# Products of the identity with a constant at five steps of a chunk inverse, in a two-block transformer kernel

## The reference, cut to what matters

```python
def step(S, inp):
    w_t, k_t, v_t, a_t, b_t = inp[:5]
    sa = jnp.einsum('bhij,bhj->bhi', S, a_t)
    S = S * w_t[:, :, None, :] + sa[..., None] * b_t[:, :, None, :] + v_t[..., None] * k_t[:, :, None, :]
    y = jnp.einsum('bhij,bhj->bhi', S, inp[5]) if emit else None
    return S, y
```

## Time and profile before

| | |
|---|---|
| median of 3 runs | 2728.89 us |
| lowest, highest | 2722.32, 2736.04 us |
| the profiled execution | 2728.74 us, of which the profile's span is 2726.9 us |
| PE busy | 2439.7 us (89% of the span) |
| DVE, ACT, POOL busy | 943.1, 509.3, 133.9 us |
| the recurrence's inverses, on PE | from about 1393 to 1648 us of the span |

### The profile page before, as it was taken

How to read it: one execution, slowest core, us unless ns; L and a number is a source line. 1 busy time by engine, 2 the same in 40 slices (tenths; PEclk the granted TensorE clock), 3 DMA queues, 4 the chain that set the end, 5 groups by cost and what they waited for, 6 DMA issues and landing times.

```text
span 2726.9 us, 39043 instructions
## 1 busy us (share of the span) xinstructions
PE 2439.7 (89%) x16646; PEld 1745.4 (64%) x16646; DVE 943.1 (35%) x1712; ACT 509.3 (19%) x1072; POOL 133.9 (5%) x132
## 2 busy tenths in 40 slices
PE   8999899999999899999989999999777777777776
PEld 6868678887857788887658888854333333333333
DVE  3757624223734512322566642241111111111112
ACT  3116310001126211001235321021000000000002
POOL 1310000000310000000000000100000000000000
PEclk9999999999999999999989889999788788878788
DMA  8345357555332373462000004569999999999998
GB/s 331 152 195 221 127 198 269 193 229 229 129 139 78 131 273 148 177 249 103 31 1 2 2 3 186 217 277 428 428 428 428 429 429 428 428 428 429 428 429 355
DMA packets 48782, 667.04 MB, mean 245 GB/s; under 512 B 5530, under 2 KB 5573, under 8 KB 7568
## 3 DMA queue, kind: packets, MB, share of 16 engines
q1 hardware_dynamic: 46928, 657.81, 58.8%
q0 software_dynamic: 1728, 7.38, 0.8%
HBM read 664.11 MB, written 1.05 MB: 244 GB/s over the span
## 4 chain that ended last, share of the span: by engine, by line
PE 65%; DMA 26%; DVE 6%; ACT 2%; issue 1%; POOL 0%; DVEq 0%; SPq 0%; ACTq 0%; POOLq 0%
PE bank L2842 29%; PE bank L2818 20%; DMA arena<-exp_w 14%; DMA ring<-exp_w 11%; PE bank L2826 6%; PE bank L3112 2%; PE bank L3058 2%; DVE arena L2538 1%; PE bank L2830 1%; PE bank L2086 1%; DVE hT L2694 1%; PE bank L2855 1%; PE bank L1975 1%; PE bank L2835 1%; ACT arena L2464 0%
## 5 line engine op out<-in xcount | busy, mean ns | idle before, releaser
L2842 PE MATMUL bank<-hT,ring 128*128 128x256 f32 x2880 | 641.0, 382 | 3.2 <-DMA ring<-w_mlp_up 2.6
L2842 PEld LDWEIGHTS bank<-hT,ring 128*128 128x128 f32 x2880 | 547.5, 191 | 99.8 <-issue 21.5
L2826 PE MATMUL bank<-ring,arena 128*32 128x256 f32 (+1 forms) x2944 | 307.4, 566 | 128.9 <-DMA ring<-exp_w 114.4
L2826 PEld LDWEIGHTS bank<-ring,arena 128*32 128x32 f32 x2944 | 106.5, 127 | 302.1 <-issue 198.4
L2826 PE MATMUL bank<-arena 128*32 128x512 f32 (+1 forms) x1072 | 159.1, 729 | 76.0 <-DMA arena<-exp_w 75.1
L2842 PE MATMUL bank<-arena,ring 128*128 128x256 f32 x1024 | 224.0, 380 | 1.5 <-DVE arena L2776 1.5
L2818 PEld LDWEIGHTS bank<-vec,arena 128*128 128x128 f32 x1344 | 179.0, 213 | 67.8 <-issue 67.0
L2818 PE MATMUL bank<-arena 64*128 64x128 f32 (+4 forms) x1156 | 209.9, 385 | 2.6 <-ACT arena L2447 1.6
L2842 PEld LDWEIGHTS bank<-arena,ring 128*128 128x128 f32 x1024 | 193.8, 190 | 27.8 <-DVE arena L2776 1.9
L1707 DVE COPY arena<-bank 128x512 f32<-128x512 f32 x64 | 44.3, 692 | 457.5 <-PE bank L2826 457.5
L2818 PE MATMUL bank<-vec,arena 128*128 128x32 f32 (+2 forms) x1344 | 182.9, 288 | 3.4 <-DVE arena L2538 3.4
(11 more groups left out here) (344 smaller groups left out, 2216.5 us busy)
## 6 DMA issues: line engine op xcount, KB each, us to landing
ring<-exp_w SPq DMA_DIRECT2D x124, 2048.0 KB, 26.0
arena<-exp_w SPq DMA_DIRECT2D x65, 2048.0 KB, 26.2
ring<-w_in SPq DMA_DIRECT2D x38, 2048.0 KB, 8.1
ring<-ada_w SPq DMA_DIRECT2D x24, 2048.0 KB, 7.8
ring<-w_mlp_up SPq DMA_DIRECT2D x16, 2048.0 KB, 7.9
ring<-w_mlp_down SPq DMA_DIRECT2D x16, 2048.0 KB, 8.0
ring<-mod_w SPq DMA_DIRECT2D x12, 2048.0 KB, 7.9
ring<-w_out SPq DMA_DIRECT2D x6, 2048.0 KB, 8.1
```

Source lines behind the costliest of these rows:

```text
L2826: mm = nc.tensor.matmul(o, a, b, start=(start and i < 4), stop=(stop and i >= len(pairs) - 4))
L2842: mm = nc.tensor.matmul(b[:, i * SEQ:(i + 1) * SEQ], w[:, k, j * P:(j + 1) * P], rhs(k), start=(k == 0), stop=(k == count - 1))
```

## The change

A table names four steps and how many filling products each gets, `kk` gets 4*g of them (0 for group 0, and 4 for group 1, the only other group that has a `kk`), and both call the existing `keep_busy` on the step's first bank. The filling stands behind the step's `start`, so behind the wait for its banks, and ahead of the step's other waits.

```diff
+STEPS_WITH_FILLING = {("W", 0, 3, 0): 3, ("XT", 0, 3, 0): 6, ("XT", 1, 4, 0): 4, ("T", 2, 3, 1): 4}
...
                 elif what == "kk":
                     b = start(("kk", g))
+                    keep_busy(b, 4 * g)
                     pe.wait_ge(solve_loaded, 48)
                     pe.wait_ge(kk_squared, g + 1)
...
                     banks = [start((what, g, lev, tile), i) for i, tile in enumerate(pair)]
+                    keep_busy(banks[0], STEPS_WITH_FILLING.get((what, g, lev, ci), 0))
                     if what == "W":
```

## The result

The changed kernel takes 2737.7 us (median of 20 runs, 2731.2 to 2749.0), against 2729.1 us (20 runs, 2718.8 to 2737.4): 1.0033 times before, interval 1.0022 to 1.0044. That is 9.0 us slower by the ratio (6.0 to 12.0): a loss clear of the scatter between runs, and smaller than 0.5%. The profiled execution of the changed kernel took 2742.88 us, 5 us above its median, so not each of its 14.2 us over the profiled one of before stands for the kernel.

The account below looks back on a forecast made before the run. It took PE and what PE waits for to bound the kernel up to about 1900 us, and weight DMAs in the experts. Terms 3.6 + 1.4 - 4.6 + 3.4 = +3.8 us on 2728.74 gave 2732.5, range 2722 to 2745.

Parts of the forecast that it names:

- XT(0,3,0) stands behind its wait: Six products start only after the 3.66 us bank wait, at the low clock; +3.6 us together with W(0,3,0), at most +5.3.
- W(0,3,0): Three products fill the wait for POOL's identity; the clock doesn't fall at 1409.1, and this chain moves 0.9 us earlier.
- kk(1): Four products start 0.6 us before kk did and end 3.0 us late; +1.4 us if they hold the clock, else +3.0.
- XT(1,4,0): Four products move W(1,5,1)'s 2.15 us wait under the filling; the 13.5 us low stretch needn't begin: -4.6 us, else +1.5.
- T(2,3,1): Four products stand behind the wait for RB(2,0)'s banks; +2.9 us if the clock holds, +4.5 if it falls, taken +3.4.
- Reaching the end: A microsecond on PE in the recurrence is one on the end; the experts begin later by as much.
- Rival 3: Experts bound by DMA, their weights not held up by PE's progress, so the end stays: 2729 us; chance 8%.
- My last sign of being wrong: The forecast is wrong if the recurrence's end moves by another amount than the run's end.
- Rival 1: Filling at full price, the clock falling all the same at 1480.8, 1545.4 and 1497.9: +14.3 us, 2743; chance 22%.
- Rival 2: The clock gives back more: one or both long low stretches after XT6 go, 5 to 6 us each: 2722; chance 20%.
- no bias: Low stretches after XT6 may go or also come in group 0, so the forecast left them out.
- read by busy time alone: The low stretch after W(1,5,1) would end after some 3 us, leaving 1.6 us to win, not 6.1; total 4.5 us higher.

Follow-up runs that it names:

- e2_behind_banks: Only the three fillings behind bank waits, XT(0,3,0) 6, kk(1) 4, T(2,3,1) 4, added to the kernel before: 2741.97 us against 2730.1, ratio 1.0045.
- e1_xt14_only: Only the four filling products at XT(1,4,0), added to the kernel before: 2724.95 us against 2730.1, ratio 0.9983.
- e8_xt14_again: Second timing of the kernel with only the four products at XT(1,4,0), against the kernel before: 2725.34 us against 2729.57, ratio 0.9978.
- e6_thin: At XT(1,4,0) alone, 45 thin 64x64 products in place of the four dense ones, against the kernel before: 2726.71 us against 2729.61, ratio 0.9989.
- e7_xt6_only: Only one product at XT6 of chunk 0 in each of four groups, added to the kernel before: 2722.29 us against 2729.61, ratio 0.9969.

## Why the prediction was right, and which terms were off

It said 2732.5 us, a small loss within 0.5%, in 2722 to 2745; the median is 2737.7.

- **XT(0,3,0) stands behind its wait.** Right: it starts at 1423.61, where 1423.6 was forecast, after 4.68 us of idle time. **The term is mis-sized**: +5.2 with W(0,3,0), not +3.6. The step that failed is "I let the clock come back about 2.6 us into it": in the profile of the change the clock stayed low to 1429.7, 6.1 us into the filling, and it took 8.42 us and not 6.8. That was the bound given, +5.3. `e2_behind_banks` had the filling at 7.08 us, 1.3 us less, which would make this term 3.9. My 3.6 lay just below both that were seen.
- **W(0,3,0).** Right: no fall at 1409.1, W(0,3,1) takes 1.15 us (1.0 forecast), and DVE's masks and so XT(0,3,0)'s banks come 0.9 us earlier. It wasn't run alone.
- **kk(1).** Right: +1.4 as forecast; its idle time is 2.14 us instead of 2.72, since the filling needs only the bank and not ACT's squares. The profile's releaser (DVE) was not what kk itself waited for last. The clock didn't fall. That the filling held it isn't shown: of the seven profiles with an unfilled wait of 2.72 us at kk(1), the clock fell behind it in five and stayed up in two, `e1_xt14_only` and `e8_xt14_again`. Part of this term can be luck.
- **XT(1,4,0).** Right: -4.1, forecast -4.6. The 0.5 us are an inconsistency of mine: I counted the three steps ahead of W(1,5,1) as 3.0 us in group 1 (96 records in a row of their own) but as 3.7 us in group 2 (96 of 160 records). From XT(1,4,0) to XT6 it is 14.65 us (1506.47 to 1521.12), and in group 2 before 14.5, so the pattern itself held.
- **T(2,3,1).** The mechanism was right, **the term mis-sized**: +4.9, not +3.4. I stood between a clock that holds (+2.9) and one that falls (+4.5); it fell, in the profile of the change and in `e2_behind_banks`, with 5.37 us for four products in both. One us of dense products at the end of a 2 us gap didn't hold it. The choice between the two was a guess: behind the unfilled wait the clock fell in five of seven profiles and stayed up in `e6_thin` and `e7_xt6_only`.
- **Reaching the end.** Right: from the gates to the last experts nothing is taken up; the experts begin 12.3 us late and the span is 14.2 us longer. Rival 3 falls. My last sign of being wrong, that the recurrence's end and the run's end move by different amounts, did appear in this pair: 9.3 against 14.2 us. 3 us of that arise in the router and 2 in the experts, where nothing is changed, and the medians differ by 8.6; I had left no room for how the clock scatters there.
- **Rival 1** (every filling at its price, +14.3) fails at XT(1,4,0) and kk(1), but is right in its other two terms (5.3 and 4.5, measured 5.2 and 4.9). **Rival 2** (other long stretches go) came in group 2 and was made up for in groups 0 and 3: in the change's profile they sum to +1.9. That there was "no bias" fits, but `e7_xt6_only` shows that the stretches weren't chance to be left alone. At the recurrence's end the 9.3 us of the profiles are the forecast's 3.8, 3.1 from the two mis-sized terms, 0.5 at XT(1,4,0) and this 1.9.

The page "TensorE: Matmul & The Clock Gate" of the Trainium skill (Part 1, What's actually happening), read by busy time alone, gave a total 4.5 us higher than forecast, near what was measured. That is by accident: it leaves nothing to win at XT(1,4,0) (1.6 less the filling's 1.5), where the traces show 4.1 us won, and what made the total higher were the terms above. At this point the measurement decides: 13.5 of 13.5 us busy at the low clock.

## What to carry to other kernels

Filling wins the idle time that it takes the place of, and the low stretch that then doesn't begin. Behind the wait for its own bank it cost its time, 12 us for 14 products, and at W(1,5,1) it only paid for itself by the traces. Before adding it, look which wait ends the idle time and whether the filling's own bank needs the same wait; if it does, put the filling one step earlier, into banks that are free, ahead of a result that nobody needs yet. And count the stretches at the low clock, not the length of the gaps: a gap of 1.0 us at XT6 was followed by 13.5 us at the low clock, one of 2.0 us at T(2,3,1) by 3.5 us or by nothing, and one product of 1 us closed the shorter one. Why the shorter gap costs more isn't shown. One profile doesn't tell where the clock will fall, so look at several before placing a filling.

## What the runs showed of the hardware

- After a gap, steps of 64x64 pieces ran 13.5 us at the low clock while PE was busy all the time, and the same steps ran at the full clock when the gap was filled, with 128x128 products or with thin ones (18.57 of 19.70 us busy at 1.00). But they don't simply go on at the level at which they begin: behind kk(1) and behind XT6 of group 1 the clock came back after 3.1 and 3.3 us, at XT6 in steps of 64x64 and 64x128 pieces alone. What decides how long it stays low isn't shown.
- The length of a gap doesn't tell whether the clock falls behind it: waits of 2.72 us at kk(1) and of 1.98 us at T(2,3,1) were each followed by a low stretch in five profiles of seven, gaps of 0.8 to 1.0 us at XT6 in 27 of 35.
- Dense products don't bring it back at once: of six at XT(0,3,0) the first 6.1 us ran at the low clock in the changed kernel, and the first 3.4 us in `e2_behind_banks`.
- A product of the identity with 512 float32 columns took 0.90 to 0.91 us at the full clock (3.60 us for four, 4.56 for five); six of which the first 6.1 us lay at the low clock took 8.42.
